# Last head's state products inside the output projection, and other places for a state read-out, bank rings and a table load

## The reference

```
def step(S, inp):
    qc, kc, fc, vc = inp
    A = jnp.cumsum(fc, axis=2)
    inter = jnp.einsum('bhtk,bhkv->bhtv', qc * jnp.exp(A), S)
    ...
    S_new = jnp.exp(A_end[:, :, 0, :])[..., None] * S + jnp.einsum('bhsk,bhsv->bhkv', kc * jnp.exp(A_end - A), vc)
    return S_new, inter + intra
...
o = _head_norm(o, hg_gn, False) * jax.nn.silu(gp.astype(f32))
return jnp.einsum('ble,ed->bld', o.astype(h.dtype), w_out), s_new
```

## Time and profile before

| | |
|---|---|
| median of three runs | 1481.58 us (1480.04 to 1482.13) |
| the profiled execution | 1482.85 us, its span 1481.0 us |
| mean granted clock of TensorE | 0.994 of full speed |
| busy: PE, DVE, ACT, POOL | 98%, 78%, 63%, 6% of the span |
| stages (us from the span's start) | layer 0 heads to 209, projection and dense part to 480, layer 1 heads to 669, projection to 700, router to 716, experts to the end |

### The profile page before, as it was taken

One profiled execution on the slowest core, in us unless ns is written; L12 is line 12 of the kernel. 1 busy time (PEld: TensorE's weight loads), 2 busy tenths in 40 slices (PEclk: granted clock), 3 DMA queues, 4 the chain that ended last, 5 costly groups with the idle time before them and its releaser, 6 DMA issues.

```text
span 1481.0 us, 23131 instructions
## 1 busy us (share of the span) xinstructions
PE 1455.0 (98%) x8514; PEld 1288.9 (87%) x8514; DVE 1148.0 (78%) x1283; ACT 936.2 (63%) x983; POOL 82.4 (6%) x97
## 2 busy tenths in 40 slices
PE   9999999999999989999999999999999999999997
PEld 8889889999999989888888888888888888888885
DVE  5766687554556697776888988989889888898997
ACT  5354755334334675363877878778787787877875
POOL 1023100000001000120300000000000000000011
PEclk9999999999999999999999999999999999999999
DMA  8578636996456523542999999999999999999994
GB/s 233 143 144 144 126 101 186 309 297 186 122 143 193 167 86 105 154 128 75 408 408 409 410 365 393 366 401 391 357 392 364 401 387 364 393 376 385 394 344 163
DMA packets 213733, 404.06 MB, mean 273 GB/s; under 512 B 13487, under 2 KB 130507, under 8 KB 213534
## 3 DMA queue, kind: packets, MB, share of 16 engines
q1 hardware_dynamic: 203120, 373.62, 72.2%
q0 software_dynamic: 6320, 22.21, 5.0%
q10 hardware_dynamic: 4222, 7.26, 1.3%
HBM read 372.76 MB, written 30.28 MB: 272 GB/s over the span
## 4 chain that ended last, share of the span: by engine, by line
PE 89%; DVE 6%; ACT 2%; issue 1%; DMA 1%; POOL 1%; SPq 0%; DVEq 0%; ACTq 0%; POOLq 0%
PE bank L536 26%; PE bank L538 26%; PE bank L537 26%; PE bank L1234 1%; PE bank L830 1%; PE bank L1048 1%; POOL expert_rows L2796 1%; DVE dense_lo L1982 1%; PE bank L793 1%; DMA ring<-in_w_in_ab 1%; PE bank L763 1%; DVE w_lo L2494 1%; PE bank L704 1%; ACT dense_hi L1462 1%; DMA expert_rows<-arena,IDX 0%
## 5 line engine op out<-in xcount | busy, mean ns | idle before, releaser
L2494 DVE TENSOR_TENSOR w_lo<-arena,w_hi 128x2048 fp32r<-128x2048 f32 (+1 forms) x280 | 596.7, 2166 | 76.3 <-ACT w_hi L1823 75.5
L1823 ACT ACTIVATE w_hi<-arena 128x2048 fp32r<-128x2048 f32 (+1 forms) x280 | 501.8, 1820 | 116.0 <-PE bank L538 105.2
L536 PE MATMUL bank<-w_hi,xg_hi 128*128 128x512 f32 x704 | 275.6, 391 | 0.5 <-DVE w_lo L2494 0.3
L538 PE MATMUL bank<-w_hi,xg_lo 128*128 128x512 f32 x704 | 274.1, 389 | 0.0
L537 PE MATMUL bank<-w_lo,xg_hi 128*128 128x512 f32 x704 | 274.0, 389 | 0.0
L1982 DVE TENSOR_TENSOR dense_lo<-ring,dense_hi 128x2048 fp32r<-128x2048 f32 (+1 forms) x77 | 165.6, 2150 | 127.6 <-ACT dense_hi L1462 127.6
L1462 ACT ACTIVATE dense_hi<-ring 128x2048 fp32r<-128x2048 f32 (+1 forms) x78 | 140.5, 1802 | 136.0 <-PE bank L538 110.5
L536 PEld LDWEIGHTS bank<-w_hi,xg_hi 128*128 128x128 f32 x704 | 132.2, 188 | 30.8 <-issue 3.1
L538 PEld LDWEIGHTS bank<-w_hi,xg_lo 128*128 128x128 f32 x704 | 132.1, 188 | 27.6
L537 PEld LDWEIGHTS bank<-w_lo,xg_hi 128*128 128x128 f32 x704 | 132.2, 188 | 26.9
L536 PE MATMUL bank<-h_hi,dense_hi 128*128 128x320 f32 x448 | 143.2, 320 | 3.3 <-DVE h_lo_a L2052 1.8
(11 more groups left out here) (474 smaller groups left out, 2333.0 us busy)
## 6 DMA issues: line engine op xcount, KB each, us to landing
arena<-in_w_moe_down SPq DMA_DIRECT2D x176, 512.0 KB, 6.8
arena<-in_w_moe_gate SPq DMA_DIRECT2D x128, 512.0 KB, 7.7
arena<-in_w_moe_up SPq DMA_DIRECT2D x128, 512.0 KB, 7.4
arena<-in_w_moe_gate SPq DMA_DIRECT2D x64, 384.0 KB, 4.2
arena<-in_w_moe_up SPq DMA_DIRECT2D x64, 384.0 KB, 5.2
ring<-in_w_in_ab SPq DMA_DIRECT2D x32, 512.0 KB, 8.7
ring<-in_w_in_c SPq DMA_DIRECT2D x32, 512.0 KB, 4.6
expert_rows<-ZERO SPq DMA_DIRECT2D x12, 1024.0 KB, 7.7
```

The lines of the kernel that those rows point to most:

```text
L536: mm(out, left[0], right[0], start=start, stop=False)
L538: return mm(out, left[1], right[0], start=False, stop=stop)
L1823: fn(WH[SLOT_OF[p]][:, 0:unit_size(p)], STAGE[:, s, 0:unit_size(p)], ACT.Copy).then_inc(S("unit_hi"), 1)
L2494: v.tensor_tensor(WL[w][:, 0:n], STAGE[:, s, 0:n], WH[w][:, 0:n].bitcast(F32), ALU.subtract).then_inc(S("unit_split"), 1)
```

## The change

In `C_STEPS`, `thin` of head 7 moves from behind the states of head 6 to right behind the output of head 6, ahead of the square of head 6, the last two silus and the scalings of heads 0 to 3. Output 7 and its square move ahead of the gates of heads 4 and 5, gate 6 ahead of the scalings of heads 4 and 5. The scalings and parts of heads 6 and 7 come ahead of the last weight split of VectorE (`wl`) and of the states of head 7, which are now the last name. TensorE's share of these states (`LAST_STATE`) leaves the list: it is issued in `projection_out`, after six of the eight blocks, and its two banks for the samples come from ScalarE's ring. VectorE reads them after a new wait for ScalarE's copy of the prompt state. Three of the four bank rings begin elsewhere. In layer 0, ScalarE's load of the square-root table moves from ahead of the prompt state of head 7 to behind the high part of head 3.

```diff
-    turn6 gate2 gate3 state5 turn7 g7 along out6 sq6 silug1 silug2 mixc0 mixc1 mixc2 mixc3 state6 thin7 h0 h1 h2 h3 gate4
-    gate5 mixc4 mixc5 out7 sq7 gate6 h4 h5 varc1 rootc1 gate7 state7 wh wl mixc6 mixc7 h6 h7
+    turn6 gate2 gate3 state5 turn7 g7 along out6 thin7 sq6 silug1 silug2 mixc0 mixc1 mixc2 mixc3 state6 h0 h1 h2 h3 out7 sq7 gate4
+    gate5 gate6 mixc4 mixc5 h4 h5 varc1 rootc1 gate7 wh mixc6 mixc7 h6 h7 wl state7
...
+        LAST_STATE = (1, KD - 1)
...
-        rings = {"act": (0, 4, 0), "dve": (4, 4, 1), "tail_act": (0, 3, 0), "tail_dve": (3, 5, 0)}
+        rings = {"act": (0, 4, 0), "dve": (4, 4, 3), "tail_act": (0, 3, 1), "tail_dve": (3, 5, 2)}
...
+                kind = "act" if (layer, u) == LAST_STATE else "dve"
                 for g in range(2):
-                    b = open_bank("dve")
+                    b = open_bank(kind)
...
-                            close_bank("dve", ins, ("ss", layer, u, g))
+                            close_bank(kind, ins, ("ss", layer, u, g))
...
+                    if kind == "oc" and k == HEADS[1][0]:
+                        state_prompt(*LAST_STATE)
+                        for _ in state_samples(*LAST_STATE):
+                            pass
...
-                elif name == "state":
+                elif name == "state" and (1, u) != LAST_STATE:
...
                 elif name == "state":
-                    if u == KD - 1:
-                        nc.scalar.preload_act_table_set("sqrt_and_others")
                     prompt_state(0, u)
...
                     mixed_high("mix0", OR, u)
+                    if u == H4 - 1:
+                        nc.scalar.preload_act_table_set("sqrt_and_others")
...
                 dve.wait_ge(S(f"state_in_{STATE_SLOT[u]}"), 16 * state_turn(layer, u))
+                if (layer, u) == LAST_STATE:
+                    after_empty(dve, ("sp", layer, u))
```

More of the change, by code:

```diff
@@ L1955, in take @@
                 kind, n = ticket[name]
-                assert kind in ("dve", "tail_dve") or "scale" in name
+                assert kind in ("dve", "tail_dve") or "scale" in name or name[:3] == ("ss", *LAST_STATE)
                 held["kind"] = kind
```

## The result

The kernel after took 1484.44 us (median of 15 runs, 1483.25 to 1491.61), the kernel before, run beside it, 1481.10 us (15 runs, 1478.12 to 1484.16). The ratio of the times, round by round, is 1.0029 with a 95% interval of 1.0022 to 1.0037: 4.3 us slower, between 3.3 and 5.5. The forecast was 1484.6 us.

A forecast was written before the change was run, and what follows sets the result against it. TensorE, busy 1455.0 of 1481.0 us, was taken to bound the kernel. New waits, less those removed, delay the second layer's seventh projection block by 3.06 us: 1481.58 + 3.06 = 1484.6 us, range 1480.6 to 1486.0.

The forecast's parts named there:

- Part 1, the wait at `thin7`: Second layer: TensorE reaches thin7 at 659.42 and waits 3.73 us for head 7's state load.
- ScalarE's chain as the second wait: Second layer's variance: TensorE waits again, 1.43 us, for ScalarE, whose work on head 7's square follows thin7's late copy.
- the clock falls too: Rival, chance 0.19: TensorE's clock also falls with the new second-layer wait; 1481.58 + 3.96 = 1485.5 us.
- The sum: Second layer's seventh projection block starts at 680.42 against 677.36, +3.06 us, giving 1484.6 us for the kernel.
- Part 2, state products between the blocks: Second layer's projection: moved state products hide the scalings of heads 6 and 7; the 1.23 us wait goes.
- the state there in time: Rival, chance 0.18: thin7 starts at 659.42, seventh block 0.67 us earlier, 1480.9; without ScalarE's chain 1.86 us, 1479.7.
- Part 3: First layer's projection: the 0.78 us bank wait goes, but head 0's low part holds TensorE; gain 0, table load 0.

The follow-up runs named there:

- second profile: The kernel after, unchanged, profiled once more in a single run to look at the clock again; 1488.15 us.
- experiment 2: The kernel before, with only thin7 moved to right behind output 6; 1490.07 us, ratio 1.0059 to before.
- Experiment 4: The kernel after, with eight unread products keeping TensorE at work ahead of thin7's wait; 1482.40 us, ratio 1.0019 to before.
- experiment 3: The kernel after, with head 7's state in head 3's slot, free earlier, so its load is issued earlier; 1479.03 us, ratio 1.0008 to before.
- experiment 1: The kernel after, with thin7 put back behind the states of head 6; 1477.87 us, ratio 0.9984 to before.
- experiment 5: experiment 3 with thin7 listed behind square 6 and the two silus, so ScalarE copies it after them; 1480.45 us, ratio 0.9998 to before.
- experiment 7: experiment 1 with output 7 and its square back behind the scalings of heads 4 and 5; one run, 1479.09 us.
- experiment 6: experiment 1 with the first layer's states of head 7 listed behind the parts of heads 0 to 3; 1478.90 us, ratio 0.9988 to before.

## Why the prediction was right, and where not

- *Part 1, the wait at `thin7`*: right in place, cause and size. Forecast 3.73 us from TensorE's arrival to `thin7`'s start; 3.90, 3.79 and 3.94 were measured (after, its second profile, experiment 2), of which the profiles count 3.74, 3.62 and 3.78 as idle. Experiment 4 names the load as the releaser, experiment 3 takes it away by an earlier load, experiment 1 by the place in the list. The point that decided was the 0.14 us by which `thin7` came after its data before: the store and the load on GpSimd's queue stayed where they were.
- *Part 1, ScalarE's chain as the second wait*: the step "it waits a second time, 1.43 us" did not come true in the kernel after, where TensorE itself was late at half clock: ScalarE was done with the square of head 7 at 668.94, TensorE started the variance at 669.06. The mechanism was right: at full clock, in experiments 3 and 4, the wait is there with 1.14 us, and experiment 5 removes it by the order of ScalarE's list. Where it shows, the forecast of the stretch holds to within 0.1 us: variance's second half 671.93 - 659.42 = 12.51 us after TensorE's arrival, 12.57 in experiment 4; seventh block 21.00, measured 21.03. That it is so close is partly luck: `thin7` started 0.17 later than forecast, and the way from there to the variance was 0.11 shorter.
- *The clock*: the mis-sized term. I left it out of the sum and gave "the clock falls too" a chance of 0.19 at +0.9 us. It fell in or right behind each of the three profiled waits. Against experiment 4, whose wait is the same, it cost 22.99 - 21.03 = 1.96 us in the one profile of after and 21.87 - 21.03 = 0.84 in the other. The terms of the larger: `thin7` and the scalings 5.44 us against 2.85 (+2.59); from the variance to the projection 0.41 against 2.00, since the slower TensorE no longer meets the wait for ScalarE (-1.59, 1.14 of it idle); and 0.96 of small ones behind, 0.33 of it idle for the reciprocal. So my 0.9 was the small case. The chance was too low on rows that were at hand. I wrote that the clock falls once in the second half, at the router, and that waits of up to 1.23 us had no fall. But layer 1, which begins at 480 us, has two longer waits in the trace of before with a fall right behind them (PE, then windows):

```profile
526.91 1.87 PE L1048 MATMUL bank<-arena 128*128 128x128 f32 x8 [1.59 <-DVE arena L2373]
...
614.56 1.16 PE L1048 MATMUL bank<-arena 128*128 128x128 f32 x8 [1.95 <-DVE arena L2373]
```

```profile
525.00:530.00 5.00, 3.41 (x17) 3.22 (x17) 4.38 (x14) 2.01 (x2) 0.00 (x0) 0.72 0.20 66
616.00:618.00 2.00, 2.00 (x11) 1.88 (x10) 2.00 (x4) 0.00 (x0) 0.00 (x0) 0.50 0.86 250
```

- *The sum*: 3.06 forecast, 3.93 and 5.05 in the two profiles, 3.3 to 5.5 by the times. The median lies on the forecast, 1484.44 against 1484.6, but by 3.34 us between the medians, while the ratio says 4.3: the mechanism that ran was the rival "the clock falls too" (1485.5), and the hit on the median is partly luck. The 3.06 lies below the interval of 3.3 to 5.5, and the three runs that the forecast started from had a median 0.48 above that of the fifteen.
- *Part 2, state products between the blocks*: right. They hide head 6's and 7's scalings (1.23 us gone); the second weight split began at 677.73 and the later blocks didn't wait for it. Experiments 1 and 7 show what that is worth without the wait: 1.35 us. I had put "the state there in time" at 0.67 us faster, or 1.86 if ScalarE's chain didn't count. Both came in the stretch: 0.70 in experiment 3, and 2.16 in experiment 1, where the silus no longer stand behind the copy.
- *Part 3*: right. The first layer's 0.78 us went and came back at the low part (0.93), 8.61 against 8.64. The table load in layer 0 shows no effect apart from that; it was not tried alone.

What stays open: whether the shorter stretch of experiments 3 and 5 is there in the whole time. That experiment 3 loses it in another place, in a part of its executions, is only argued from the granted clocks.

## What to carry to other kernels

Before moving an instruction ahead in an in-order list, look up when its data lands, not whether it has ever waited: a margin of 0.14 us is a consumer that came by chance just in time. Price a new wait of TensorE with its own length, the in-order engines behind it, and the half clock that follows it; if the wait can't be moved away, products that nobody reads save the last part. Test the edits of a bundle one by one: here one moved name turned a gain of 2.4 us into a loss of 4.3, and the best version is experiment 1, faster than both kernels (experiment 6, which adds to it, can't be told from it).

## What was not expected of the hardware

The time at half clock after one and the same wait (3.6 to 3.8 us with TensorE empty) ranged from 3.4 to 6.8 us, and the fall came inside the wait in one execution, just behind its end in two. Much shorter waits can have a fall behind them, but not every time. One and the same wait of 1.59 us for VectorE near 526 us had one in four of the ten profiles (before, experiments 1, 2 and 6); the next long one, near 613, had one in five of the six profiles in which it was 1.78 to 2.00 us, and in none of the four in which it was 1.08 to 1.19. A wait of 1.79 us in experiment 2 had one too, 1.23 us in before none. The fall near 97 us in before had no wait of even 1 us within the 80 us ahead of it. And falls at places that the change doesn't touch (at 90 to 105, 520 to 530 and 610 to 620 us) were in one profiled execution and not in the other, which made the two spans differ by some 4 us ahead of the change.
